# Halving the probability buffer of a latent attention, taking its evacuations one step earlier and its query rotation two steps earlier

## The reference, cut to what matters

```python
def mla_branch(c_q, c_kv, k_r, q_gain, w_uq, kv_gain, w_ukv, cos, sin):
    q = (rms_norm(c_q, q_gain) @ w_uq).reshape(bsz, s, MLA_HEADS, QK_DIM)
    q = jnp.concatenate([q[..., :NOPE_DIM],
                         apply_rope(q[..., NOPE_DIM:], cos[:, :, None], sin[:, :, None])], axis=-1)
    kv = (rms_norm(c_kv, kv_gain) @ w_ukv).reshape(bsz, s, MLA_HEADS, NOPE_DIM + V_DIM)
    k_nope, v = kv[..., :NOPE_DIM], kv[..., NOPE_DIM:]
    k_rope = apply_rope(k_r, cos, sin)
    k = jnp.concatenate([k_nope, jnp.broadcast_to(k_rope[:, :, None], (bsz, s, MLA_HEADS, ROPE_DIM))], axis=-1)
    ...
    def attend(q_blk):
        scores = jnp.einsum('bqhd,bkhd->bhqk', q_blk, k, preferred_element_type=jnp.float32)
        p = jax.nn.softmax(scores, axis=-1)
        return jnp.einsum('bhqk,bkhd->bqhd', p.astype(v.dtype), v)
```

## Time and profile before

| what | value |
|---|---|
| three runs | 2762.81, 2764.15, 2768.38 us (median 2764.15) |
| profiled execution, its own time | 2768.38 us |
| profiled execution, its span | 2766.6 us |
| busy in the span | TensorE 2651.1 us (96%), weight loads 1987.1, VectorE 988.4, ScalarE 823.3, POOL 785.0 |
| latent attention's loop over pairs | from about 643 to 802 us |
| TensorE's granted clock in pair 2 | 1.00 |

### The profile page before, as it was taken

The page is one execution under the profiler, slowest core; times in us unless marked ns, Lnnn a source line. Parts: engine busy times, 40 slices in busy tenths (PEclk is TensorE's granted clock), DMA queues, the critical chain, the costliest instruction groups (busy, mean ns, idle before and its releaser), DMA issues.

```text
span 2766.6 us, 35416 instructions
## 1 busy us (share of the span) xinstructions
PE 2651.1 (96%) x14470; PEld 1987.1 (72%) x14470; DVE 988.4 (36%) x1800; ACT 823.3 (30%) x1439; POOL 785.0 (28%) x633
## 2 busy tenths in 40 slices
PE   7999999999999996999999799999999999999998
PEld 4877777885568883444444597988888997988887
DVE  3655665533422133212222497310011686300012
ACT  3444443433432221000000326422222337322232
POOL 2222233310114300000000242444455442444454
PEclk9999999999999997999999999999999999999999
DMA  7122212012113325999999521223223221232321
GB/s 267 54 69 81 70 61 61 31 35 69 50 36 123 122 90 230 379 420 420 420 419 419 194 92 46 77 77 106 92 92 106 77 77 47 82 102 91 102 97 46
DMA packets 212565, 382.39 MB, mean 138 GB/s; under 512 B 10833, under 2 KB 145877, under 8 KB 211413
## 3 DMA queue, kind: packets, MB, share of 16 engines
q1 hardware_dynamic: 211088, 379.06, 37.6%
q10 hardware_dynamic: 1349, 1.51, 0.2%
HBM read 378.44 MB, written 2.10 MB: 138 GB/s over the span
## 4 chain that ended last, share of the span: by engine, by line
PE 83%; DMA 8%; DVE 3%; ACT 3%; issue 1%; DVEq 1%; SPq 0%; ACTq 0%; POOL 0%; PEld 0%; PEldq 0%
PE bank L1566 14%; PE bank L1571 14%; PE bank L1570 14%; PE bank L1826 7%; PE bank L1334 5%; DMA ring<-in_w_up 4%; DMA ring<-in_w_gate 3%; PE bank L1771 2%; PE bank L1714 2%; PE bank L1368 2%; PE bank L1430 2%; PE bank L1439 1%; PE bank L1620 1%; PE bank L1443 1%; PE bank L1349 1%
## 5 line engine op out<-in xcount | busy, mean ns | idle before, releaser
L684 POOL TENSOR_TENSOR w_lo<-ring,w_hi 128x512 fp32r<-128x512 f32 x448 | 603.5, 1379 | 1462.9 <-ACT w_hi L732 1462.9
L732 ACT ACTIVATE w_hi<-ring 128x2048 fp32r<-128x2048 f32 (+1 forms) x114 | 215.0, 1886 | 669.8 <-PE bank L1566 669.7
L1566 PE MATMUL bank<-hT_hi,w_hi 128*128 128x512 f32 (+1 forms) x928 | 353.0, 380 | 2.9 <-DVE conv_acc L2710 1.6
L1571 PE MATMUL bank<-hT_hi,w_lo 128*128 128x512 f32 (+1 forms) x928 | 348.5, 376 | 0.0
L1570 PE MATMUL bank<-hT_lo,w_hi 128*128 128x512 f32 (+1 forms) x928 | 348.3, 375 | 0.0
L1826 PE MATMUL bank<-ring,xeT 128*64 128x512 f32 x992 | 225.3, 596 | 21.0 <-DMA ring<-in_w_gate 11.1
L1566 PEld LDWEIGHTS bank<-hT_hi,w_hi 128*128 128x128 f32 x928 | 175.2, 189 | 35.7 <-DVE conv_acc L2710 2.7
L1571 PEld LDWEIGHTS bank<-hT_hi,w_lo 128*128 128x128 f32 x928 | 175.1, 189 | 32.0
L1570 PEld LDWEIGHTS bank<-hT_lo,w_hi 128*128 128x128 f32 x928 | 175.2, 189 | 30.5 <-issue 1.0
L1826 PEld LDWEIGHTS bank<-ring,xeT 128*64 128x64 f32 x992 | 75.4, 136 | 146.5 <-issue 144.5
L2803 DVE TENSOR_TENSOR ffn_hT<-ffn_sg,bank 128x512 f32<-128x512 f32 x44 | 30.2, 687 | 414.8 <-PE bank L1571 414.8
(11 more groups left out here) (490 smaller groups left out, 4842.2 us busy)
## 6 DMA issues: line engine op xcount, KB each, us to landing
ring<-in_w_gate SPq DMA_DIRECT2D x86, 1024.0 KB, 8.4
ring<-in_w_down SPq DMA_DIRECT2D x86, 1024.0 KB, 13.6
ring<-in_w_up SPq DMA_DIRECT2D x82, 1024.0 KB, 13.6
ring<-in_w_in SPq DMA_DIRECT2D x33, 1024.0 KB, 5.2
head_w<-in_w_in SPq DMA_DIRECT2D x32, 512.0 KB, 4.9
mod_w<-in_w_mod SPq DMA_DIRECT2D x8, 2048.0 KB, 7.6
ring<-in_w_out SPq DMA_DIRECT2D x12, 1024.0 KB, 4.7
ring<-in_w_mod SPq DMA_DIRECT2D x8, 1024.0 KB, 14.9
```

Of the source, the lines that this page charges most:

```text
L684: last = pool.tensor_tensor(w_lo[m % 2][:, cs], src[:, cs], w_hi[m % 2][:, cs].bitcast(F32), ALU.subtract)
L732: return act.activation(dst, src, ACT.Copy)
L1566: first = mm(dst, a[0], b[0], start=start, stop=False)
L1571: return mm(dst, a[1], b[0], start=False, stop=stop)
```

## The change

Three things change in the latent attention, and nothing elsewhere.

- `probs` has two slots in place of four, so tile n uses slot `n % 2`. Exponential n waits for `turn(n - 2)` where it waited for `turn(n - 4)`.
- ScalarE evacuates tile n - 1 behind exponential n, for n from 1 to 6, where it evacuated tile n - 2 for n from 2 to 7. Tiles 6 and 7 are still evacuated behind the loop.
- VectorE does `row_max(7)`, then `rotate_q(i + 1)`, and then `normalise(6)` and `normalise(7)`. Before, the rotation stood behind both.

```diff
-        probs = r("probs", [P, 4, SEQ])
+        probs = r("probs", [P, 2, SEQ])
@@ ScalarE
                 for n in range(8):
                     act.wait_ge(sem("nmax_ready"), i * 8 + n + 1)
-                    if n >= 4:
-                        act.wait_ge(sem("p_turned"), i * 8 + n - 3)
-                    act.activation(probs[:, n % 4, :], bank[n % 4][:], ACT.Exp, scale=scale, bias=nmax[:, n % 2:n % 2 + 1],
+                    if n >= 2:
+                        act.wait_ge(sem("p_turned"), i * 8 + n - 1)
+                    act.activation(probs[:, n % 2, :], bank[n % 4][:], ACT.Exp, scale=scale, bias=nmax[:, n % 2:n % 2 + 1],
                                    accum_out=psums[:, n % 2:n % 2 + 1]).then_inc(sem("exp_done"), 1)
-                    if n >= 2:
-                        evac_probs(n - 2)
+                    if 1 <= n < 7:
+                        evac_probs(n - 1)
@@ TensorE, turn(n)
-                        last = pe.transpose(bank[4 + n % 2][:, k * P:(k + 1) * P], probs[:, n % 4, k * P:(k + 1) * P], ident[:])
+                        last = pe.transpose(bank[4 + n % 2][:, k * P:(k + 1) * P], probs[:, n % 2, k * P:(k + 1) * P], ident[:])
@@ VectorE
-                    ts(probs[:, n % 4, :], probs[:, n % 4, :], pinv[:, n % 2:n % 2 + 1], None, ALU.mult).then_inc(sem("p_ready"), 1)
+                    ts(probs[:, n % 2, :], probs[:, n % 2, :], pinv[:, n % 2:n % 2 + 1], None, ALU.mult).then_inc(sem("p_ready"), 1)

                 row_max(0)
-                for n in range(8):
-                    if n < 7:
-                        row_max(n + 1)
+                for n in range(6):
+                    row_max(n + 1)
+                    normalise(n)
+                    if i == 1:
+                        src_lo(o_dn_lo, oT_dn, o_dn_hi, 0, (n,))
+                row_max(7)
+                if i + 1 < HEADS // 2:
+                    rotate_q(i + 1)
+                for n in (6, 7):
                     normalise(n)
                     if i == 1:
                         src_lo(o_dn_lo, oT_dn, o_dn_hi, 0, (n,))
                 if i + 1 < HEADS // 2:
-                    rotate_q(i + 1)
                     take_rope_and_v(i + 1)
```

## The result

The changed kernel takes 2783.72 us (median of 6 runs, 2782.46 to 2789.14) where the kernel before takes 2765.55 in the same comparison (6 runs, 2762.81 to 2769.59): 18.2 us more, ratio 1.0069 with a 95% interval from 1.0058 to 1.0081. It was forecast 10.4 us slower, with a range that ended at 2779. The direction is right; the time lies outside the range, and the change is 1.7 times the forecast one. The profiled execution took 2787.93 us, 4.2 above the median, and spans 2786.1, 19.5 more than before's profiled one.

What follows compares the result with a forecast made beforehand. TensorE was taken as the bound, waiting ahead of scores(3) for ScalarE's order between turn(0) and exponential 3. Terms 5.2 + 2.2 + 3.0 = 10.4 us on the median 2764.15 gave 2774.5; range 2769 to 2779.

Steps and rivals of the forecast that it cites:

- the falling clock as a rival: Idles ahead of scores(3) in pairs 1 and 2 drop TensorE to 1.2 GHz: 3.5 us more, 2778; chance 0.13.
- Front stalls: Longer TensorE waits ahead of scores(3) in all four pairs, exponential 3 being late: 5.2 us together.
- turn(5): New TensorE wait at turn(5) in pairs 1 and 2, their splits queued behind evacuation 2: 2.2 us, ends 0 and 3.
- Rotation: Rotation ahead of normalisations 6 and 7 delays turn(6) and turn(7) in pairs 1 and 2: 3.0 us, ends 0 and 5.
- the prediction's own sign for a forecast too low: A prediction too low would come of POOL's splits stretching the rotation on VectorE; rotation's upper end 5 us.
- Buffers: Halving probs costs 0 by itself in the new order; in the old order 0.67 per pair, 2.7 us in all.
- What lies behind: After the attention no transfer with a fixed start absorbs the delay, so all of it passes through to the end.
- That only the front stalls show: Rival: VectorE and project_q(0) hide the rest, leaving 5.2 us more, 2769.4; chance 0.12.
- the delay is absorbed: Rival: the expert weights' stream behind the attention absorbs the 10.4 us, time stays 2764; chance 0.07.
- The third: The rival that TensorE's clock falls behind idles in pairs 1 and 2: 3.5 us more, 2778; chance 0.13.

Runs made afterwards that it cites:

- experiment 1: Changed kernel with unread matmuls filling TensorE's waits ahead of scores(3) and of turns 5, 6 and 7: 2780.9 us against 2768.19 of before, ratio 1.0049.
- experiment 2: Kernel before with one wait made longer, scores(3) waiting for exponential 4 and not 3: 2777.15 us against 2768.96, ratio 1.0032.
- experiment 8: Changed kernel with the splits of pairs 1 and 2 ahead of the evacuation of the same step: 2779.51 us against 2768.8 of before, ratio 1.0045.
- experiments 4 and 5: Kernel before with the evacuation moved alone, four slots: 2777.63 us, ratio 1.0033; changed kernel with the rotation back behind normalisation 7, two slots: 2779.87 us, ratio 1.0043.
- experiment 6: Kernel before with two slots of probs alone, old order of evacuations and rotation: 2771.35 us against 2768.19, ratio 1.0016.
- experiment 9: Kernel before with turn(0) ahead of scores(2) in pairs 0 to 2: 2763.01 us against 2768.96, ratio 0.9977.
- experiment 7: Kernel before with the rotation alone moved ahead of normalisations 6 and 7: 2770.17 us against 2768.19, ratio 1.0009.

## Why the prediction was wrong in size and right in kind

**The failed step** is the clock. The forecast took all work at 2.4 GHz, on the ground that an idle of 1.86 us had left the clock of pair 2 at 1.00, and gave the falling clock as a rival 0.13, at 3.5 us, from two falls. The profile had four falls, 17.1 us at 1.2 GHz, up to 8.5 us. Filling the idles takes the falls away and leaves 12.7 (experiment 1); making the idles without the edit brings falls (experiment 2). The row that I had against the rival was of a shorter idle than those to come, and the row for it, 3.75 us with a fall, a longer one; in between I took the side that was cheaper. The trace of before had rows in between, which the prediction does not use. Behind an idle of 2.33 us the clock fell:

```profile
1546.07 0.76 PE L1796 MATMUL bank<-ye_hi,scat_now 128*128 128x512 f32 x1 [2.33 <-DVE ye_lo L2590]
...
1546.00:1547.00 1.00, 0.93 (x2) 0.83 (x3) 0.58 (x1) 1.00 (x3) 0.00 (x0) 0.51 0.60 215
```

At L1940 it fell behind 1.74 us (at 1729.03) and not behind 1.68 (at 2327.48). So the forecast's ground, that 1.86 us had left the clock alone once, said little even of that length. That rival's two idles were forecast as 3.1 each and measured 3.13 and 3.02: the step from idle to clock was wrong, not the idle. Its price was too small as well, 3.5 us from two falls where the profile has up to 8.5 from four, and so was its 2778. The waits are 1.0 over the forecast, and 1.4 of the distance of the absolute time from 2774.5 is the scale (before's median is 2765.55, not 2764.15). The Trainium skill, TensorE: Matmul & The Clock Gate, section HAM oscillation, says that a TensorE left idle between bursts drops to its lower clock and starts the next one slow. The runs agree in kind, at the price above; the section's own case has waits of about 3 to 5 us, while here falls also followed idles of 2.08 and 2.30.

**Front stalls:** 5.2 forecast, 9.6 - 4.4 = 5.2 measured. Exponential 2 and evacuation 1 between evacuation 0 and exponential 3 is what the timeline shows.

**turn(5):** 2.2 forecast, 1.01 + 1.46 = 2.5 measured, in pairs 1 and 2 alone, and gone with the splits moved (experiment 8).

**Rotation:** 3.0 forecast, 3.7 measured. The three waits of pair 1, at turn 5, 6 and 7, came out within 0.3 us. Pair 2 was undersized: 1.37 and 0.75 for 0.48 and 0.45, and 1.46 for 1.08 at turn 5. Both terms of VectorE's work were too short there: one step of the rotation and the normalisation behind it take

```profile
761.19 1.08 DVE L2375 TENSOR_TENSOR qr_tok<-rope_t 128x256 f32<-128x256 f32 x1
...
764.09 1.00 DVE L2429 TENSOR_SCALAR probs<-probs,pinv 128x512 f32<-128x512 f32 x1
```

where pair 1 has 0.43 and 0.49 and I had 0.74 for the second. POOL's eight `w_lo` instructions run from 755.43 to 766.2. In the same pair the last two normalisations before 755.43 take 0.49 and the four from then on 0.69, 1.23, 1.00 and 1.26. That fits the prediction's own sign for a forecast too low, POOL stretching VectorE's work; no run takes POOL's work away, so it stays argued.

**Buffers:** 0 in the new order (experiments 4 and 5 have the same waits), 2.7 forecast for the old order and 3.0 measured (experiment 6).

**What lies behind:** the delay passes through: stretch 20.8, span 19.5. The 1.3 between them fit the 3.3 us less at 1.2 GHz outside the attention, up to 1.6. That `scores(3)` waits for ScalarE's order and "not for a free buffer" was put too strongly: exponential 3 has to free its PSUM bank first. With `turn(0)` moved up, the bank is free before TensorE asks for it (experiment 9); whether one more bank would do it too was not tested.

**The rivals.** That only the front stalls show, is out, as L1631 waits 6.2. That the delay is absorbed, is out. The third came true, in more places than it named and not always.

**Left open.** Waits and half of the time at 1.2 GHz make 19.9 of the stretch's 20.8. The six new waits at the turns, at the 0.28 of experiment 7 each, would add 1.7, a little more than is missing; half of the time at 1.2 GHz is the most that it can cost. In the filled kernel, without a fall, 11.4 of 12.8 are waits and the same 1.7 would fit. What decides whether the clock falls at one and the same idle stays open too.

## What to carry to other kernels

When an edit lengthens TensorE's waits, add the clock to the price: the waits here were reckoned to 1 us, and the change was out by 7.8, mostly because matmuls behind an idle of 2 to 3 us may run at half speed for 3 us and more. Look for idles of the length to come in the whole trace and not beside the edit alone: the one of 2.33 us stood in it. Before moving work on one engine, ask what the neighbour's list makes it wait for: the gap was in the order of TensorE's list, and moving the turn of one tile ahead of a block of scores in three pairs took away 4.2 of the 4.4 us of waits, where three moves on the engines around it only added to them.

## What the hardware showed that I had not expected

The clock fell behind shorter idles than I had thought, and not always. Over the ten profiles with idles left and no fill, for idles ahead of `scores(3)` in pairs 0 to 2: none of 9 idles from 0.92 to 1.87 us was followed by a fall; 3 of 8 from 2.07 to 2.30 were; 12 of 13 from 2.59 to 3.97 were. A stretch at 1.2 GHz then mostly lasted about 3.4 us (1.7 lost), at times twice that. It also fell behind several short idles in a row (1.37 and 0.75 at turn 6 and 7 of pair 2) in two of the three profiles that have them in that form. Pair 3's idles of 1.38 were never followed by one. These counts hold for this place: at L1940, later in the same traces, idles of 1.68 to 1.74 were followed by a fall in some cases and not in others.
